# First block's attention: two of four heads' probabilities scaled by ScalarE, the factors made at the beginning of an iteration

## The reference, cut to what matters

```python
s_c = einsum('bqkgd,bnkd->bqkgn', qc, k_cmp) * scale
p_c = masked_softmax(s_c, mask_c);  o_c = einsum(..., p_c, v_cmp)
...  # p_s, o_s with k_slc, v_slc;  p_w, o_w with k_win, v_win
return gc[..., 0:1] * o_c + gc[..., 1:2] * o_s + gc[..., 2:3] * o_w
```

## Time and profile before

| | |
|---|---|
| median of 3 runs | 2876.6 us (2875.53 to 2876.87) |
| the profiled execution | 2878.09 us, span 2876.0 us |
| granted TensorE clock, mean | 0.971 of full speed |
| TensorE matmul busy | 2700.5 us (94%) |
| VectorE busy | 1277.6 us (44%) |
| ScalarE busy | 424.4 us (15%) |
| GpSimd busy | 191.3 us (7%) |
| DMA | 634.94 MB, mean 221 GB/s |

### The profile page before, as it was taken

One profiled execution on the slowest core, in us unless ns is written; L12 is line 12 of the kernel. 1 busy time (PEld: TensorE's weight loads), 2 busy tenths in 40 slices (PEclk: granted clock), 3 DMA queues, 4 the chain that ended last, 5 costly groups with the idle time before them and its releaser, 6 DMA issues.

```text
span 2876.0 us, 48956 instructions
## 1 busy us (share of the span) xinstructions
PE 2700.5 (94%) x20613; PEld 1712.4 (60%) x20613; DVE 1277.6 (44%) x3014; ACT 424.4 (15%) x995; POOL 191.3 (7%) x240
## 2 busy tenths in 40 slices
PE   7789999978899999999999998899989999998998
PEld 5557994755433333333333367579657966865993
DVE  1874676386311101111111155546665665334666
ACT  1131000113010110111101111400041001023100
POOL 1700000060000000000000010100000000032000
PEclk9879999988999999999999999999999999999999
DMA  8644555554499999999999964345514544222452
GB/s 275 193 162 147 163 175 175 192 177 147 191 347 393 381 412 394 382 410 388 400 398 379 407 210 98 56 141 167 176 59 132 165 173 132 73 74 71 150 172 93
DMA packets 274370, 634.94 MB, mean 221 GB/s; under 512 B 15161, under 2 KB 148673, under 8 KB 257648
## 3 DMA queue, kind: packets, MB, share of 16 engines
q1 hardware_dynamic: 268688, 616.09, 58.9%
q0 software_dynamic: 4800, 13.56, 2.6%
q10 hardware_dynamic: 672, 2.22, 0.2%
HBM read 623.98 MB, written 7.84 MB: 220 GB/s over the span
## 4 chain that ended last, share of the span: by engine, by line
PE 85%; DVE 11%; issue 2%; ACT 1%; DMA 0%; PEld 0%; DVEq 0%; PEldq 0%; ACTq 0%
PE pacc L1095 13%; PE pacc L1169 10%; PE pt L901 9%; PE pt L1169 7%; PE pt L1095 6%; PE pacc L1133 6%; PE pacc L1195 5%; PE pt L1195 5%; PE pacc L1036 4%; PE po L1169 3%; PE pt L1133 3%; DVE bigc L2542 3%; PE pt L1536 2%; PE pt L1074 2%; PE pacc L939 2%
## 5 line engine op out<-in xcount | busy, mean ns | idle before, releaser
L2294 DVE TENSOR_TENSOR gateb<-kT,pt 128x512 f32<-128x512 f32 (+1 forms) x32 | 19.9, 622 | 477.5 <-PE pt L1169 476.8
L1169 PE MATMUL pacc<-ring,bigc 128*32 128x512 f32 (+1 forms) x1920 | 188.6, 550 | 4.5 <-issue 3.1
L901 PE MATMUL pt<-ring,hT 128*128 128x256 f32 x832 | 190.7, 389 | 2.2 <-DVEq L1887 1.9
L901 PEld LDWEIGHTS pt<-ring,hT 128*128 128x128 f32 x832 | 160.9, 195 | 29.9 <-issue 6.8
L1095 PE MATMUL pacc<-probT,prob 128*128 128x128 f32 x1440 | 170.6, 275 | 0.0
L1095 PEld LDWEIGHTS pacc<-probT,prob 128*128 128x128 f32 x1440 | 165.6, 192 | 0.0
L1169 PEld LDWEIGHTS pacc<-ring,bigc 128*32 128x32 f32 x1920 | 68.3, 110 | 123.1 <-issue 121.1
L1169 PE MATMUL pt<-ring,bigc 128*32 128x512 f32 (+1 forms) x1280 | 139.5, 550 | 0.0
L1195 PE MATMUL pacc<-ring,bigc 128*32 128x512 f32 x864 | 137.9, 595 | 0.0
L1133 PE MATMUL pacc<-prob,chunks 128*128 128x512 f32 x282 | 136.3, 592 | 0.0
L2111 DVE TENSOR_TENSOR prob<-ring 128x512 f32<-128x512 f32 x86 | 59.5, 692 | 153.3 <-PE pacc L1095 107.0
(11 more groups left out here) (427 smaller groups left out, 4412.3 us busy)
## 6 DMA issues: line engine op xcount, KB each, us to landing
ring<-in_moe_w_down SPq DMA_DIRECT2D x80, 1024.0 KB, 14.0
ring<-in_w_gate_up SPq DMA_DIRECT2D x66, 1024.0 KB, 5.1
ring<-in_w_ada SPq DMA_DIRECT2D x48, 1024.0 KB, 5.4
ring<-in_moe_w_gate SPq DMA_DIRECT2D x48, 1024.0 KB, 6.3
ring<-in_moe_w_up SPq DMA_DIRECT2D x48, 1024.0 KB, 16.7
ring<-in_w_down SPq DMA_DIRECT2D x33, 1024.0 KB, 4.9
ring<-in_moe_w_gate SPq DMA_DIRECT2D x32, 768.0 KB, 12.5
ring<-in_moe_w_up SPq DMA_DIRECT2D x32, 768.0 KB, 8.8
```

Of the source, the lines that this page charges most:

```text
L901: ins = pe.matmul(t[:, q * 256:q * 256 + n], src[:, k, q * P:q * P + P], w[:, k, 0:n], start=(k == 0), stop=(k == KC - 1))
L1169: ins = pe.matmul(((X, Y, Z) if kind == "g" else up_bank)[r][32 * j:32 * j + 32, 0:w], hcurv[:, kc, 32 * g:32 * g + 32], moe_view(tile_)[: ...
```

## The change

Two new semaphores, `prob_scaled` and `shares_made`. VectorE makes the factors of batch i+1 at the beginning of iteration i instead of behind `probT_ready`, tells ScalarE when they are there, and scales heads 0 and 1 only. ScalarE scales heads 2 and 3 with a Copy activation whose scale is the factor, batch 0 behind the first eight exponentials, batch i+1 as the first thing of iteration i. TensorE's `turn` waits for both. The second block's attention has no gates and takes none of these paths.

```diff
+SCALED_BY_VECTOR = 2
@@ TensorE, turn(i)
                         pe.wait_ge(prob_ready, due("prob_ready"))
+                        pe.wait_ge(prob_scaled, due("prob_scaled"))
@@ ScalarE, exps
+                def scale(i):
+
+                    b = batches[i]
+                    act.wait_ge(shares_made, due("shares_made"))
+                    for j in range(SCALED_BY_VECTOR, 4):
+                        o = b.prob_at(i, j)
+                        ins = act.activation(prob[:, o:o + b.nk], prob[:, o:o + b.nk], ACT.Copy,
+                                             scale=den[:, 24 + (i % 4) * 4 + j:25 + (i % 4) * 4 + j])
+                    ins.then_inc(prob_scaled, 1)
...
+                gated = batches[0].gate is not None
+                if gated:
+                    scale(0)
                 for i, b in enumerate(batches):
+                    if gated and i < last:
+                        scale(i + 1)
@@ VectorE, shares(i)
-                    for j in range(4):
+                    ve.sem_inc(shares_made, 1)
+                    for j in range(SCALED_BY_VECTOR):
                         o = b.prob_at(i, j)
                         go(ve.tensor_scalar(prob[:, o:o + b.nk], prob[:, o:o + b.nk], den_[:, j:j + 1], None, ALU.mult))
                     tell(prob_ready)
@@ VectorE, attention
                 for i, b in enumerate(batches):
+                    if gated and i < last:
+                        shares(i + 1)
                     if 1 < i + lead <= last:
                         shift(i + lead)
...
                     if not gated:
                         shares(i)
-                    elif i < last:
-                        shares(i + 1)
                     if conv is not None:
                         conv(i)
```

More of the change, by code:

```diff
@@ L289, in build @@
         prob_ready = sem("prob_ready")
+        prob_scaled = sem("prob_scaled")
+        shares_made = sem("shares_made")
         odd_copied = sem("odd_copied")
```

## The result

| | median (range), 10 runs each | of before |
|---|---|---|
| before | 2877.7 us (2873.8 to 2879.4) | |
| changed | 2885.3 us (2880.2 to 2890.5) | 1.0030, 95% interval 1.0020 to 1.0039 |
| predicted | 2878.3 us (2873.5 to 2881.5) | |

A forecast was written before the change was run, and what follows sets the result against it. Inside the two attention stretches the bound alternates between VectorE and TensorE, partly at half clock. Layer 0 +0.4, layer 1 +0.7 and a clock term +0.6 gave +1.7 us on 2876.6: 2878.3 us, range 2873.5 to 2881.5.

The forecast's parts named there:

- Turn(0): First batch's transposes: start 0.9 us later, as ScalarE's scaling stands behind exp(1).
- Output(3): Zeroing matmul gated by VectorE: moves -0.35 us in layer 0, about -0.1 in layer 1; kept as -0.3 and 0.
- Output(6): Iteration 6: the next batch's factors and scalings go ahead of its release, so it starts 1.2 us later.
- ScalarE's copy: Scaled Copy costs as much as an exponential, a pair 0.5 us at 15 keys, 0.9 at 256; no table load.
- Two clock falls: TensorE's clock falls twice per layer's attention, at the same work as before.
- The deciding term: Iteration 6: turn(7) stands behind the zeroing and output matmuls and starts 0.75 to 1.75 us later; taken as +1.25.
- The section on the clock: Long TensorE idle ahead of output(3) and output(6) brings slow stretches; the first idle stays, the second grows a microsecond.
- +0.6 for even odds: Layer 1: a later turn(7) may lose the early return of the clock, 1.15 us at even odds.
- Outside them no instruction changes: The change touches only the attention stretches of layers 0 and 1, some 70 us each, 5% of the span.
- A: ScalarE's hand-over becomes the gate and the clock returns later in both layers: +7 us, 2883.6; chance 0.08.
- B: Removed waits at turn(3), (7), (11) and the end count in full: -4.2 us, 2872.4; chance 0.2.
- C: A slow stretch behind output(3) disappears in each layer: -8 us, 2868.6; chance 0.05.

The follow-up runs named there:

- the order alone: Changed kernel, but VectorE does all four scalings, with the factors at the beginning of the iteration, and ScalarE scales nothing: 2884.5 us.
- the split alone: Changed kernel, but the factors stay at the end of the iteration and ScalarE scales two heads behind its exponentials: 2877.5 us.
- late masks: GpSimd builds its first mask three results later in the second block's first attention: 2882.5 us in the changed kernel, 2877.2 in before.
- the best one: Changed kernel with factors and ScalarE's scaling back at the end in iterations 3, 6 and 9, and GpSimd's masks held back: 2870.9 us.
- the shift behind the factors: Kernel before, with VectorE's shift(i+2) moved from the beginning of a gated iteration to behind the factors: 2882.8 us.
- split, shift behind the factors: Scalings split with ScalarE, factors at the iteration's end, shift behind them, probT_odd released ahead of the exponentials: 2872.7 us, 0.9989 of before.
- two copies ahead: Kernel before with two idle four-column VectorE copies ahead of one addition in the second block's first attention: 2879.5 us.
- late where a result is copied: Changed kernel, but in iterations 3, 6 and 9 factors and ScalarE's scaling go back to the end: 2873.9 us.
- changed, again: The changed kernel run a second time, nothing altered: 2882.2 us, 1.0017 of before.
- the last nudged kernel: Kernel before with four idle four-column VectorE copies ahead of one addition in the second block's first attention: 2883.3 us.

## Why the prediction was wrong

**What held.** Turn(0) +0.7 (forecast +0.9). Output(3) +0.1 and +0.3 (-0.3 and -0.1, so 0.4 too early in each layer): VectorE's saved scalings were spent on the earlier factors. Output(6) +1.3 and +1.6 (+1.2). No wait for VectorE's scalings ahead of turn(3), (7) and (11). ScalarE's copy costs an exponential, without a table load. Two clock falls in each layer. Both stretches between 71 and 73 us. The scheme of the attention stood, and the medians show that the moved order is what costs: the order alone is 6.8 us above before, the split alone not at all, and with late masks the old order back in three iterations takes 11.6 off.

**What was mis-sized.** The deciding term, turn(7) behind the zeroing and output matmuls, had bounds of +0.75 and +1.75, and I took the middle. It came out at +1.8 and +2.0, just beyond the upper end, and those matmuls run at half clock: the zeroing pair took 1.22 us, against 0.70 in the earlier trace rows. The section on the clock had expected slow matmuls behind each such wait, but its reading of the first fall was wrong: the earlier trace rows has 0.53 in 168 to 171 us, and the matmuls from 167.96 on took 1.79 us for 1.07, ahead of the 2.41 us of idle time. It also had that idle time as unchanged, and it grew to 3.73. In layer 1 the clock came back later within batch 7, +2.7 us at output(7) where I had +0.6 for even odds. Over the profiles at hand, the changed attention takes 71.96, 71.87 and 72.05 us in layer 0 and 72.44, 72.42 and 72.45 in layer 1; the unchanged one takes 71.60, 71.61, 71.46 and 68.51, and 70.27, 70.28, 70.27 and 70.23. The means differ by 1.2 and 2.2 us: +3.4 where the sum said +1.7. Layer 0's 1.2 hangs on the single 68.51; without it the difference is 0.4, just what the sum had for that layer. That was luck: turn(7) came half a microsecond later than I had it, and the clock was back sooner behind it (5.1 us from turn(7) to output(7), 5.8 before). Layer 1 had +1.3 in the sum and got +2.2. So the stretches give 2.6 to 3.4 us, and they alone would have ended at 2879 to 2880, inside the range.

**The step that failed** is the sentence "Outside them no instruction changes", from which I took it that no time changes outside them, and so put everything else in the sum at nothing. Two places outside them cost time in the profiles.
- The second block's first attention. In the two profiles of the changed kernel the distance grows by 6.8 and 4.7 us there, and making a collision by hand in before costs 6.0 in the median. But taking it out by late masks changed no median clearly (by 2.8 less to 0.3 more in the changed kernel, 3.0 less in the best one, 0.6 less in before). Its share of the changed kernel's median is thus not shown: how many of the unprofiled executions collide, and whether the clock hits them alike, can't be seen. The kernel with late masks is still 4.7 us above before, and the split alone, which had the collision in its profile, isn't slower than before: theory 2, by which most of the loss is the collision, isn't borne out.
- The router of layer 1, +1.4 us. Its 16 matmuls take 3.08 to 3.79 us in the nine profiles of the changed kernel and of what was built on it, and 2.05 in the five of before and of what was built on that, the one with the shift behind the factors among them. So it goes with the change, but with which part isn't told apart: the order alone has it as the split alone has. Why the clock falls there is open.

Stretches and router together are 2.6 to 3.4 plus 1.4, or 4.0 to 4.8 us, against +4.7 with late masks, +6.2 over all runs of the changed kernel and +7.6 in the first comparison. What is left, 1.4 to 3.6 us, fits a collision in some of the executions, but that is argued and not shown. These are terms of different kinds (means of stretches, one profile, differences of medians and means), and for the kernel with the order alone such a sum doesn't close: 6.6 in its stretches and 1.7 in the router are already 8.3, where its median rose by 6.8. Its profile has 4.4 more in the second block's first attention, and 3.0 less around 1690 us.

**The rivals.** A (slower: the hand-over is the gate, clock back later) was right in layer 1 on two of its terms, turn(7) and the clock, and wrong in its condition: VectorE had no slack ahead of output(3), and turn(0)'s delay was absorbed. It reached 2883.6 through terms of which half occurred. B's gains came (the waits did go), but the release of output(6) took more. C, a slow stretch that disappears, came true in no run of the changed kernel.

**The chances.** 0.06 for slower rested on a sum for 5% of the span, while the other 95% had an error of its own that I had set to nothing. A range that allowed for one such overlap would have reached 2880 plus some 5 us, about 2885, which is where the first comparison ended.

**What stays open** is why the addition came late at all. The additions follow each other every 7.09 us, in untouched code. In the changed kernel this one comes after 7.46, with a gap of 0.51 us behind the last read of the accumulator, where 0.15 is usual; with late masks, and so with no GpSimd work beside it, the gap is the same. Before had such a long gap at another instruction, the 0.62 us of the earlier trace rows. With the order alone, which has as many VectorE instructions as before (3014), the stall sits one addition earlier (7.44 us, then 7.10), and the addition beside GpSimd is as late by it. So VectorE has rare stalls of about 0.37 us that stay at one place from profile to profile of a kernel, and an edit can move them even where it leaves the number of instructions as it was. That is a reading of the traces; no run was made that moves the stall alone.

## What to carry to other kernels

Work moved to the start of an iteration goes ahead of everything that the iteration releases: look for the iterations with an extra copy or wait in them (3, 6 and 9 here), price the move there, and if need be keep the old order in those alone (-4 us in each layer's stretch here). Before an edit is called local, list where VectorE and GpSimd run within half a microsecond of each other anywhere in the program, as a shift of 0.3 us can turn a free overlap into one after which the profiles here fall 4 to 7 us behind. Where TensorE's clock falls after an idle time, take the upper end of every term that follows it: the same eight transposes took 1.97 us here where they take 1.09 at full clock. And before a wait is read as the cause of a fall, look whether the matmuls ahead of it were slow already.

## What the runs showed of the hardware

*An operation of GpSimd holds up a small one of VectorE until its own end.* The lag is the start of a four-column addition on VectorE minus the start of GpSimd's 2.00 us operation, for the first such meeting of each kernel and, in the last two rows, for a second one:

| kernel | lag, us | the addition took, us |
|---|---|---|
| shift behind the factors, on before | -0.70 | 0.16 |
| before | -0.28 | 0.16 |
| split, shift behind the factors | -0.23 | 0.16 |
| two copies ahead | -0.11 | 0.16 |
| split alone | +0.01 | 2.00 |
| changed | +0.03 | 1.99 |
| changed, again | +0.14 | 1.87 |
| order alone | +0.18 | 1.84 |
| late where a result is copied | +0.50 | 1.51 |
| changed, at 1839.18 | +0.40 | 1.61 |
| before, at 1833.61 | +0.99 | 1.04 |

In each row with a positive lag the two durations end together: lag and duration make 2.0. Between -0.11 and +0.01 the price goes from nothing to all of it. The Trainium skill, "SBUF — State Buffer", section "Who interferes with whom", says that a VectorE instruction with two SBUF inputs contends with a GpSimd one that reads SBUF, that whichever comes first keeps the shared pair for its whole instruction, and that the other blocks fully. The runs agree in each row with GpSimd first. Where VectorE was first it was done within 0.05 us of GpSimd's start, so nothing here shows what GpSimd would lose. The four-column copy with one input, caught in the last nudged kernel (2.71 us for four), agrees with the same section's statement that a copy can enter a mode that contends; by that profile alone.

*The clock's phase is part of the time of unchanged code.* The kernel before with four copies added far behind has the same first block as before, and its layer 0 stretch took 68.51 us against 71.60. The kernel with late masks and the late order had 68.14 us in one layer and 65.11 in the other. Around 1690 us, in code of the second block that is alike in all these kernels, the 20 us from 1680 on run at a clock of 0.83 in before. In the kernel that is late where a result is copied, the same work took 17 us at 1.00. Four of the 14 profiles have this gain of 3.0 us (order alone, split alone, late where a result is copied, split with the shift behind the factors), and why these four isn't known. The single stretch of one profile is therefore good to some 3 us only. The runs of one kernel spread over 4 to 14 us, and how much of that is the clock isn't shown.
